# Input turned before its norm, narrow products merged, and the odd mixer's rotations and squares on GpSimd, in a two-block network of split fp32 products

## The reference

```python
h = rms_norm(x, norm_mix_pre); proj = h @ w_in          # recurrent and attention inputs, gates, indexer
xr, gr, q, k, v, iq, ik, iw, g_a, g_b = split(proj)
y_rnn = rg_lru(conv(xr), ...) * gelu(gr)                 # linear recurrence over the tokens
q, k, iq, ik = rope(...)                                 # indexer picks the 64 best keys of each query
merged = sigmoid(g_a) * (y_rnn @ w_rnn_out) + sigmoid(g_b) * (y_att @ w_att_out)
x = x + rms_norm(merged @ w_o); x = x + rms_norm(swiglu(rms_norm(x)))
# second block: swiglu, even mixer, swiglu, swiglu, odd mixer, swiglu
proj = rmsnorm(x, od_norm) @ od_w_in                     # odd mixer
c_q, c_kv, k_pe, gq, gk, gv = split(proj)
q = rope(rmsnorm((rmsnorm(c_q) @ w_uq)));  kv = rmsnorm(c_kv) @ w_ukv    # "d": 8 heads of 96
qd, kd = axial_rope(rmsnorm(gq)), axial_rope(rmsnorm(gk))                # "c": 8 heads of 64
mix = concat([attention(q, k, v_c), attention(qd, kd, vd)]) @ od_w_out
```

## Time and profile before

| what | us |
|---|---|
| median of 3 runs (range) | 1427.22 (1423.85 to 1429.24) |
| the profiled execution's own time | 1423.9 |
| its span | 1422.1 |
| PE busy | 1393.8 (98%) |
| PE weight loads | 1173.7 (83%) |
| DVE busy | 879.7 (62%) |
| ACT busy | 770.7 (54%) |
| POOL busy | 13.0 (1%) |
| chain of work that ended last | PE 95%, DVE 2%, ACT 2% |

### The profile page before, as it was taken

The page is one execution under the profiler, slowest core; times in us unless marked ns, Lnnn a source line. Parts: engine busy times, 40 slices in busy tenths (PEclk is TensorE's granted clock), DMA queues, the critical chain, the costliest instruction groups (busy, mean ns, idle before and its releaser), DMA issues.

```text
span 1422.1 us, 18520 instructions
## 1 busy us (share of the span) xinstructions
PE 1393.8 (98%) x6978; PEld 1173.7 (83%) x6978; DVE 879.7 (62%) x1345; ACT 770.7 (54%) x1169; POOL 13.0 (1%) x21
## 2 busy tenths in 40 slices
PE   7999999999999999999999999999999989999999
PEld 6799888788887888888788888888888868888887
DVE  6889846665545755557976555565555674565543
ACT  5589844554545544445765444454444576554441
POOL 2000000000000000000000000000000000000000
PEclk9999999999999999999999999999999989999999
DMA  8453556476655566566346655666655431366651
GB/s 298 142 161 106 160 166 182 144 216 184 190 180 168 187 186 185 182 189 205 113 155 196 190 180 191 183 189 180 188 182 189 145 118 59 106 212 187 191 180 60
DMA packets 131767, 242.57 MB, mean 171 GB/s; under 512 B 8544, under 2 KB 21472, under 8 KB 131680
## 3 DMA queue, kind: packets, MB, share of 16 engines
q1 hardware_dynamic: 130768, 239.15, 54.7%
q0 software_dynamic: 624, 2.10, 0.5%
q10 hardware_dynamic: 288, 0.14, 0.0%
HBM read 240.31 MB, written 1.05 MB: 170 GB/s over the span
## 4 chain that ended last, share of the span: by engine, by line
PE 95%; DVE 2%; ACT 2%; issue 0%; DMA 0%; SPq 0%; ACTq 0%; DVEq 0%
PE PB L345 28%; PE PB L347 27%; PE PB L346 27%; PE PB L391 5%; PE PB L616 2%; PE PB L505 2%; PE PB L339 1%; PE PB L341 1%; PE PB L340 1%; DVE WL L318 1%; PE PB L509 0%; DMA X<-in_x_dram 0%; DVE XC L783 0%; PE PB L797 0%; PE PB L986 0%
## 5 line engine op out<-in xcount | busy, mean ns | idle before, releaser
L318 DVE TENSOR_TENSOR WL<-RAW,WH 128x1024 fp32r<-128x1024 f32 (+1 forms) x453 | 548.4, 1217 | 442.4 <-ACT WH L312 440.9
L312 ACT ACTIVATE WH<-RAW 128x1024 fp32r<-128x1024 f32 (+1 forms) x453 | 475.6, 1055 | 517.2 <-PE PB L347 509.0
L345 PE MATMUL PB<-WH,AT0h 128*128 128x512 f32 (+3 forms) x1328 | 507.9, 382 | 6.6 <-DVE AT0l L1232 6.5
L347 PE MATMUL PB<-WH,AT0l 128*128 128x512 f32 (+3 forms) x1328 | 497.6, 375 | 0.0
L346 PE MATMUL PB<-WL,AT0h 128*128 128x512 f32 (+3 forms) x1328 | 497.0, 374 | 0.0
L345 PEld LDWEIGHTS PB<-WH,AT0h 128*128 128x128 f32 x1328 | 250.9, 189 | 51.6 <-issue 10.1
L347 PEld LDWEIGHTS PB<-WH,AT0l 128*128 128x128 f32 x1328 | 250.7, 189 | 44.7
L346 PEld LDWEIGHTS PB<-WL,AT0h 128*128 128x128 f32 x1328 | 251.2, 189 | 44.1 <-issue 2.2
L345 PE MATMUL PB<-WH,FTh 128*128 128x512 f32 x440 | 172.1, 391 | 0.0
L347 PE MATMUL PB<-WH,FTl 128*128 128x512 f32 x440 | 171.3, 389 | 0.0
L346 PE MATMUL PB<-WL,FTh 128*128 128x512 f32 x440 | 171.2, 389 | 0.0
(11 more groups left out here) (304 smaller groups left out, 1043.0 us busy)
## 6 DMA issues: line engine op xcount, KB each, us to landing
RAW<-in_ffn_w_gu_dram SPq DMA_DIRECT2D x88, 512.0 KB, 4.0
RAW<-in_ffn_w_gu_2b_dram SPq DMA_DIRECT2D x88, 512.0 KB, 3.7
...
```

What stands on the lines that cost most here:

```text
L312: e.activation(WH[i % NHL][:, 0:m], RAW[i % NRAW][:, 0:m], ACT.Copy).then_inc(*up("hi", i))
L318: e.tensor_tensor(WL[i % NHL][:, 0:m], RAW[i % NRAW][:, 0:m], WH[i % NHL][:, 0:m].bitcast(F32), ALU.subtract).then_inc(*up("lo", i))
L345: e.matmul(o, p.src[0][:, kx, t], h[:, j:j + p.n], start=start, stop=False)
L347: ins = e.matmul(o, p.src[1][:, kx, t], h[:, j:j + p.n], start=False, stop=stop)
```

## The change

Five edits, and new hand-written orders around them.

1. **Start.** x comes in four quarters; PE turns x itself. The gain is applied in the split as before, the reciprocal root `rs_in` by whoever evacuates: as `scale` of ScalarE's copies for IQ, IKW, KV, Q0, Q1, and (halved, `hrs`) in the tanh of GA and GB. For XR and GR, whose tokens lie along the free axis, a matmul of ones with a diagonal spreads the root over all partitions (`pe_in_spread`, tile RSB in JK), and GpSimd multiplies XR and GR by it (`pool_xr`, `pool_gr`). GR is now copied, multiplied, and put through Gelu by a second ScalarE operation (`act_gelu`). The squares and the root run after the first splits.
2. **IQ and IKW** are cut at 320 and 264 columns instead of 512 and 72. A chunk holds three 128-row pieces, so there are 3 and 3 chunks instead of 4 and 1, and all later chunk numbers are one higher.
3. **Feed-forward.** The weights lie in the order gate, upper, gate, upper; group 5 is one product of 512 columns (256 gate, 256 upper in one bank) instead of two of 256. The banks of f = 1 and f = 3 swap.
4. **Odd mixer.** All rotations go to GpSimd (`pool_odd_rot`), and so do the squares of UKV and UQ; VectorE evacuates the values of UKV (`dve_uv`) and squares one block of CQ. ScalarE evacuates UKV by 4 operations instead of 12 and UQ by 4 instead of 8. `act_warm` runs one Exp on a single column early in the odd mixer.
5. **Orders.** In the first mixer `pe_gates` and attention "a" stand later among the dense passes, and in the odd mixer four passes of OO stand before attention "d". In the f1 boundary `dve_post_root(e, 'f1', 1)` stands behind two `dve_block_lo`.

```diff
-        IQ = product("w_in", 3584, 512, AT0, A)
-        IKW = product("w_in", 4096, 72, AT0, B)
+        IQ = product("w_in", 3584, 320, AT0, A)
+        IKW = product("w_in", 3904, 264, AT0, B)
...
+            for g in range(5):
+                gate.append(product(wgu, 1024 * g, 512, AT0, P, blocks=4 if by_blocks and g == 0 else 0))
+                upper.append(product(wgu, 1024 * g + 512, 512, AT0, Q, lead=LEAD if by_blocks and g == 0 else 0))
+            gate.append(product(wgu, 5120, 512, AT0, P))
...
-            for c in range(2):
-                for b in range(2):
-                    e.tensor_scalar(XN[:, b, c * 512:c * 512 + 512], X[:, b, c * 512:c * 512 + 512],
-                                    rs_in[:, b:b + 1], None, ALU.mult).then_inc(*up("xn", (c, b)))
...
+            turned(e, 4 + q, [X[:, b, t * 128:t * 128 + 128] for t in (2 * q, 2 * q + 1) for b in range(2)], "xt", q)
...
+        def pe_in_spread(e):
+            e.wait_ge(*on("rsT", ("d", 1)))
+            e.matmul(PB[7][:, 0:S], ONES, DIAG, start=True, stop=True).then_inc(*up("rsP", "t"))
+        def pool_xr(e, c, f):
+            e.wait_ge(*on("evac", ("xr", t)))
+            e.wait_ge(*on("rsb", "b"))
+            e.tensor_tensor(x, x, RSB.unsqueeze(1).broadcast_to([128, 2, S]), ALU.mult).then_inc(*up("xr_s", t))
...
+        def act_gelu(e, c, f):
+            e.wait_ge(*on("gr_s", t))
+            e.activation(x, x, ACT.Gelu_apprx_tanh).then_inc(*up("evac", ("gr", t)))
...
-        def dve_odd_rot(e, name, part):
+        def pool_odd_rot(e, name, part):
...
+        def act_warm(e):
+            e.wait_ge(*on("rs", "od"))
+            e.activation(warm, RS["od"][:, 0:1], ACT.Exp).then_inc(*up("warm", "o"))
...
-            e.activation(SQ3[:, b, c * 256:c * 256 + 256].rearrange("p (h d) -> p h d", d=64), x[:, :, 0:64], ACT.Square,
-                         scale=s).then_inc(*up("evac", (f"uks{c}", b)))
-            e.activation(V3[:, b, c * 256:c * 256 + 256].rearrange("p (h d) -> p h d", d=64), x[:, :, 64:128], ACT.Copy,
-                         scale=s).then_inc(*up("evac", (f"uv{c}", b)))
+        def dve_uv(e, c, b):
+            e.wait_ge(*on("evac", (f"uk{c}", b)))
+            e.tensor_scalar(V3[:, b, c * 256:c * 256 + 256].rearrange("p (h d) -> p h d", d=64), x[:, :, 64:128],
+                            ysc[:, 2 + b:3 + b], None, ALU.mult).then_inc(*up("uv", (c, b)))
+        def pool_uk_square(e, c, b):
+            e.wait_ge(*on("evac", (f"uk{c}", b)))
+            e.tensor_tensor(SQ3[:, b, c * 256:c * 256 + 256].rearrange("p (h d) -> p h d", d=64), x, x,
+                            ALU.mult).then_inc(*up("usq", ("k", c, b)))
```

More of the change, by code:

```diff
@@ new lines, in pe_first_mixer @@
+            pe_scores(e, AT_A, 8)
+            pe_scores(e, AT_A, 9)
+            dense(e, GA0, 7, 8)
+            pe_scores(e, AT_A, 10)
+            dense(e, GA1, 0, 2)
+            pe_turn_p(e, AT_A, 6)
+            dense(e, GA1, 2, 4)
+            pe_turn_p(e, AT_A, 7)
+            pe_values(e, AT_A, 6)
+            dense(e, GA1, 4, 6)
+            pe_turn_p(e, AT_A, 8)
+            pe_values(e, AT_A, 7)
+            pe_scores(e, AT_A, 11)
+            dense(e, GA1, 6, 8)
+            pe_turn_p(e, AT_A, 9)
@@ L3235, in scalar_program @@
             act_tables(e)
-            for c in range(2):
-                act_in_square(e, c)
             act_first_mixer(e)
@@ L3254, in vector_program @@
         def vector_program(e):
-            for c in range(2):
-                dve_in_square(e, c)
-            dve_in_norm(e)
             dve_first_mixer(e)
```

1121 lines of the change are left out of this document (599 added, 522 removed).

## The result

The changed kernel takes 1412.21 us (median of 4 runs, 1409.49 to 1413.13) where the kernel before takes 1425.76 (a fourth run of it has come in since the 1427.22 of the forecast): a ratio of 0.9889, 95% interval 0.9873 to 0.9905. The forecast was 1414.5, faster by over 0.5%. The profiled execution took 1412.74 us with a span of 1410.9, against 1423.9 and 1422.1: 11.2 us less where 12.7 were expected.

What follows compares the result with a forecast made beforehand. PE, busy 1393.8 of 1422.1 us, was taken as the bound; -6.4 - 1.7 - 2.4 - 0.5 - 4.0 + 2.3 = -12.7 us gave 1411.2 profiled, 1414.5 for the median, range 1402 to 1429 (the forecast's own case 1408 to 1421).

Steps and rivals of the forecast that it cites:

- Start, -6.4: Program start: input split earlier and IQ, IKW cheaper, so KV starts near 23.9 instead of 30.33 us; bounds -3.3 and -9.
- The loads keep up: Program start: weight chunks would land in time, with 4.4 MB instead of 4.9 MB ahead of chunk 5.
- the case that the prediction priced at 2.6 us: Program start: clock still low while IQ's first chunk runs (18 matmuls), losing 2.6 us.
- The widths' 13.0 us: Program start: IQ and IKW at 320 and 264 columns cost PE 13.0 us instead of 16.3.
- Half-clock stretch, -1.7: After IKW: the 3.41 us at half clock behind the 72-column matmuls disappear, giving back 1.7 us; bounds 0 and -1.7.
- First mixer, +2.3: First mixer: added ScalarE operations, table loads and GpSimd multiplications, partly covered by the new order, cost 2.3 us; bounds 0 and +8.
- Feed-forward, -2.4: Five feed-forwards: merged group 5 saves 0.63 us each, less 0.15 for the later gate, 2.4 in all; bounds 0 and -3.2.
- f1 boundary, -0.5: f1 boundary: block 1's root moves behind block 0's split, for which PE waits, saving 0.5 us; bounds 0 and -1.7.
- Odd mixer, -4.0: Odd mixer: PE's 4.35 us wait and some half clock go, less new waits, net 4.0 us saved; bounds -8 and +2.
- Exclusion: Odd and first mixer: VectorE and GpSimd exclude each other, adding 3.5 and 3 us, time 1421; chance 0.16.
- Slow GpSimd: GpSimd rotations, squares and multiplications: at 5 ns an element the kernel takes 1437 us, slower than before; chance 0.10.
- ScalarE as the bound of the first mixer: First mixer: all 5 us of ScalarE work and GpSimd hops land on PE, 9 instead of 2.3, time 1421; chance 0.10.

## Why the prediction was right, point by point

The sum missed the profiled difference by 1.5 us (11.2 for 12.7), and that is partly luck: the terms were off by +0.8, +1.2 and +1.6 us (start with half clock, first mixer, f1) and by -0.35, -1.1 and -0.7 (feed-forward, odd mixer, the rest), which cancel by more than half. One half-clock piece more or less is 1.7 us. The median came out 2.3 us below its 1414.5 while the profiled execution came out 1.5 above its 1411.2: with the fourth run of the kernel before, the same sum would have given 1413.1 for the median.

**Start, -6.4.** Measured -5.6 at KV's start. The times of IQ were right within 0.15 us. "The loads keep up" failed: chunk 6 held ScalarE for 3.05 us. Of IQ's 18 matmuls on the first chunk, the case that the prediction priced at 2.6 us as running at the low clock, the first few did, for some 0.5 us. The widths' 13.0 us were right (12.89 where the pace was full and nothing was waited for), and the runs show that they carried the gain, 5.66 us with the clock's share; the early input added 2.0. Each is measured with the other in place, so the two add up to more than the 7.29.

**Half-clock stretch, -1.7.** Right, and its cause is shown: with 72 columns it came back, twice as long, and the old start with the new widths is without it. Why narrow matmuls bring the clock down is not shown.

**First mixer, +2.3.** Mis-sized: 3.5, in every run that has its operations and order, within 0.05 us. The step summed 5 us of ScalarE work and called the order a cover. The old order shows what was to be covered, 11.2 us, 3.4 of them the clock's.

**Feed-forward, -2.4.** 2.75: the 0.15 us charged for the later gate never showed.

**f1 boundary, -0.5.** The failed step. The wait did shrink by 0.5 (3.25 to 2.74), but half clock now follows it: +1.1 in all. The prediction counted the wait and not what the clock does behind it.

**Odd mixer, -4.0.** 5.1. The 4.35 us went as reasoned, and what is late next is the chain that was named, from UQ's squares on GpSimd to the fifth maximum of "c"; it costs 2.29 us where 1.5 was charged. The other 1.5, for the stretches of attention "d", show in no wait: PE has none behind 1167.51. The 8.27 us of evacuations were given more weight than they have: undone in the new order they cost 1.4. The clock gave 3.4 where 1.5 was counted.

**The rivals.** Exclusion: its mechanism is there, its price isn't: 3.5 us were put on the odd mixer for a stretch where VectorE was busy 12.89 of 13.5, but the rotations had left it. Slow GpSimd: the chain of gq and gk took 3.2 ns an element (12.2 us for 3840), just short of the 3.5 from which it was to decide, and the keys came 0.51 us late. ScalarE as the bound of the first mixer: 3.5 of the 9.
